# Working the first output projection by column pairs, with three and two groups of seven products for eight

## The reference

```python
merged = jax.nn.sigmoid(gate_a) * ya + jax.nn.sigmoid(gate_b) * yb
h = h + (merged @ w_out[l]).astype(h.dtype)
z = rmsnorm(h, norm_ffn_g[l])
ff = (jax.nn.silu(z @ w_ffn_gate[l]) * (z @ w_ffn_up[l])) @ w_ffn_down[l]
h = h + ff.astype(h.dtype)
```

## Time and profile before

| | us |
|---|---|
| three runs | 2528.5, 2528.8, 2529.35 |
| median | 2528.8 |
| profiled execution, span of its instructions | 2526.1 |
| PE busy in it | 2504.1 (99%) |
| DVE busy | 1874.6 (74%) |
| ACT busy | 1342.5 (53%) |
| POOL busy | 394.0 (16%) |

### The profile page before, as it was taken

How to read it: one execution, slowest core, us unless ns; L and a number is a source line. 1 busy time by engine, 2 the same in 40 slices (tenths; PEclk the granted TensorE clock), 3 DMA queues, 4 the chain that set the end, 5 groups by cost and what they waited for, 6 DMA issues and landing times.

```text
span 2526.1 us, 32950 instructions
## 1 busy us (share of the span) xinstructions
PE 2504.1 (99%) x11871; PEld 2103.8 (83%) x11871; DVE 1874.6 (74%) x2154; ACT 1342.5 (53%) x1801; POOL 394.0 (16%) x295
## 2 busy tenths in 40 slices
PE   9999999999999999999999999999999999999998
PEld 7889888888888888888789988888888888888887
DVE  5556554555799988999966766565669889988985
ACT  5445454444555555555555554455556655665564
POOL 1001100112212300212112301031132101210121
PEclk9999999999999999999999999999999999999999
DMA  7645556575656566565656655465465566556664
GB/s 243 201 145 156 168 168 191 191 238 179 225 192 203 188 207 226 193 201 194 227 182 183 182 148 157 149 217 175 158 220 190 194 209 207 198 199 205 211 213 161
DMA packets 252754, 485.98 MB, mean 192 GB/s; under 512 B 15339, under 2 KB 38844, under 8 KB 251468
## 3 DMA queue, kind: packets, MB, share of 16 engines
q1 hardware_dynamic: 248604, 463.99, 57.5%
q0 software_dynamic: 3696, 20.00, 2.1%
q10 hardware_dynamic: 320, 0.20, 0.0%
HBM read 478.86 MB, written 5.27 MB: 192 GB/s over the span
## 4 chain that ended last, share of the span: by engine, by line
PE 93%; DVE 3%; ACT 1%; issue 1%; DMA 0%; POOL 0%; ACTq 0%; DVEq 0%; POOLq 0%
PE acc L1667 73%; PE acc L1693 6%; PE unit L1693 4%; PE unit L1721 3%; PE psO L1693 2%; PE psS L1693 2%; PE psO L1895 1%; DVE w_lo L2023 1%; PE psS L1787 0%; ACT w_hi L1382 0%; PE psS L1861 0%; PE unit L1787 0%; DVE b_sum_lo L2215 0%; DMA w_raw<-in_w_o_cross 0%; POOL rtmp L1176 0%
## 5 line engine op out<-in xcount | busy, mean ns | idle before, releaser
L2023 DVE TENSOR_TENSOR w_lo<-w_raw,w_hi 128x1024 fp32r<-128x1024 f32 (+6 forms) x570 | 690.6, 1223 | 444.8 <-ACT w_hi L1382 439.6
L1382 ACT ACTIVATE w_hi<-w_raw 128x1024 fp32r<-128x1024 f32 (+6 forms) x570 | 573.3, 1016 | 429.1 <-PE acc L1667 401.2
L1667 PE MATMUL acc<-w_hi,xT_hi 128*128 128x512 f32 (+4 forms) x2020 | 783.1, 388 | 2.3 <-DVE xT_lo L2133 1.8
L1667 PE MATMUL acc<-w_lo,xT_hi 128*128 128x512 f32 (+4 forms) x2020 | 772.0, 382 | 0.0
L1667 PE MATMUL acc<-w_hi,xT_lo 128*128 128x512 f32 (+4 forms) x2020 | 771.4, 382 | 0.0
L1667 PEld LDWEIGHTS acc<-w_hi,xT_hi 128*128 128x128 f32 x2020 | 379.4, 188 | 71.3 <-issue 3.0
L1667 PEld LDWEIGHTS acc<-w_lo,xT_hi 128*128 128x128 f32 x2020 | 379.0, 188 | 70.0
L1667 PEld LDWEIGHTS acc<-w_hi,xT_lo 128*128 128x128 f32 x2020 | 379.6, 188 | 66.1 <-issue 0.5
L2054 DVE TENSOR_TENSOR w_lo<-w_raw,w_hi 128x1024 fp32r<-128x1024 f32 (+1 forms) x204 | 294.7, 1483 | 37.5 <-ACT w_hi L1411 36.3
L1411 ACT ACTIVATE w_hi<-w_raw 128x1024 fp32r<-128x1024 f32 (+1 forms) x204 | 200.1, 1018 | 106.6 <-PE acc L1667 92.4
L1667 PE MATMUL acc<-w_hi,hT_hi 128*128 128x512 f32 x632 | 247.3, 391 | 2.1 <-DVE w_lo L2023 1.4
(11 more groups left out here) (506 smaller groups left out, 3389.0 us busy)
## 6 DMA issues: line engine op xcount, KB each, us to landing
w_raw<-in_w_in SPq DMA_DIRECT2D x168, 512.0 KB, 3.7
w_raw<-in_w_down SPq DMA_DIRECT2D x110, 512.0 KB, 4.3
w_raw<-in_w_up SPq DMA_DIRECT2D x100, 512.0 KB, 4.1
w_raw<-in_w_ffn_down SPq DMA_DIRECT2D x76, 512.0 KB, 4.6
w_raw<-in_w_ffn_gate SPq DMA_DIRECT2D x68, 512.0 KB, 4.4
w_raw<-in_w_ffn_up SPq DMA_DIRECT2D x68, 512.0 KB, 3.8
w_raw<-in_w_out SPq DMA_DIRECT2D x64, 512.0 KB, 4.1
s_raw<-in_w_up SPq DMA_DIRECT2D x28, 512.0 KB, 6.0
```

The source lines that it names most:

```text
L1382: act.activation(w_hi[:, slot, 0:kc, 0:n], w_raw[:, slot, 0:kc, 0:n], ACT.Copy).then_inc(hi_split, 1)
L1667: ins = pe.matmul(ac[t][:, 0:n], a[:, l0 + c, t * P:(t + 1) * P], w[:, slot, c, 0:n], start=start and c == 0 and m == 0, stop=stop and c = ...
L2023: dve.tensor_tensor(w_lo[:, slot, 0:kc, 0:n], w_raw[:, slot, 0:kc, 0:n], w_hi[:, slot, 0:kc, 0:n].bitcast(F32), ALU.subtract).then_inc(lo_ ...
```

## The change

The four blocks of `w_out` become two pairs (columns 0 to 1023 and 1024 to 2047), with three groups of seven products in the first pair and two in the second. The products of a group read `xT` (new argument `lhs`). A new home `EARLY` has room for the sums of weights and activations and for the common parts. POOL makes the sums of the activations during the last `w_proj_b` block (`h_sums`), ACT and DVE split them after the first tile of `w_out` (`h_split`), and `merged3` is transposed after the fourth tile instead of the third. The loads of all five groups stay in the ring of four. Of the pair's common parts, 0 and 1 stand in pair one, 2 and 3 behind the second tile of pair two. The transposes `u0` and `u1` move behind tiles 8 and 10 of pair two's 12 plain tiles (counted from zero), `u2` and `u3` behind tiles 1 and 2 of the `w_ffn_gate` block. The home `START`, the step `shared_to` and blocks with `own` set are written but used by no step of this list.

```diff
+OUT = sevens((3, 2), ("0011S01S01S01", "01S01S00001111"), home=EARLY, ring=((0, 1, 2), (0, 1)), sums="dve", lhs="xT")
...
+    g = [group_of(OUT, half, 0, DC) for half in range(2)]
     for j in range(4):
         S += block_steps("w_proj_a", 0, 8, 512 * j, 512, "yT", 0, "gate_a", 512 * j, ("ya0", "ya1") if not j else ())
         S += weave(block_steps("w_proj_b", 0, 8, 512 * j, 512, "yT", 8, "merge", 512 * j, ("yb0", "yb1") if not j else ()),
-                   [[], both(f"merged{j - 1}")] if j else [], 1)
+                   [[("h_sums", g[0], 0)] if j == 3 else [], both(f"merged{j - 1}")] if j else [], 1)
     S += [("load_x",), ("gain", 2)]
     merged = tuple(f"merged{j}" for j in range(4))
-    blocks = [make_block("w_out", 0, DC, 512 * j, 512, "xT", 0, "add", 512 * j, () if j else merged) for j in range(4)]
-    sums_ = into_norm(2, blocks, {(3, 2): 0, (3, 4): 1, (3, 6): 2})
-    S += sums_[:3] + both("merged3") + sums_[3:]
...
+    one, rest = block_pair("w_out", 0, DC, 0, merged, 0, OUT["plans"][0], g[0], {0: [("h_split", g[0])], 3: both("merged3")})
+    two, more = block_pair("w_out", 0, DC, 1024, (), 0, OUT["plans"][1], g[1],
+                           {1: rest + pieces_of_norm(2, 0), 3: pieces_of_norm(2, 1), 8: both("u0"), 10: both("u1")})
+    assert not more
+    S += one + two + pieces_of_norm(2, 2) + pieces_of_norm(2, 3)
...
-    S += out_of_norm(2, make_block(*gate(0, U_NEEDS)))
+    first = make_block(*gate(0, U_NEEDS))
+    S += after_tiles([("tile", first, k) for k in range(8)], {0: roots(2), 1: both("u2"), 2: both("u3")}) + [("evac", first, (0, 1))]
...
                     if part == 0:
                         dve.wait_ge(p1_copied, at["group"])
+                        if group["home"] == EARLY and c0 == 0:
+                            dve.wait_ge(x_again_in, 16)
```

More of the change, by code:

```diff
@@ L244, in make_block @@
 def make_block(w, k0, kc, c0, n, lhs, l0, evac, arg=0, needs=(), turn=0):
-    return dict(w=w, k0=k0, kc=kc, c0=c0, n=n, lhs=lhs, l0=l0, evac=evac, arg=arg, needs=needs, norm=NORM_OF.get(w), ahead=0, turn=turn)
+    return dict(w=w, k0=k0, kc=kc, c0=c0, n=n, lhs=lhs, l0=l0, evac=evac, arg=arg, needs=needs, norm=NORM_OF.get(w), ahead=0, turn=turn,
+                own=False)
 def tiles_in(b):
@@ L256, in block_steps, with block_pair @@
     return [("tile", b, k) for k in range(tiles_in(b))] + [("evac", b, (0, 1))]
-def block_pair(w, k0, kc, c0, needs, turn, plan, group, between={}):
-    b = [make_block(w, k0, kc, c0 + 512 * j, 512, "hT", 0, "add", c0 + 512 * j, needs, turn) for j in range(2)]
+def block_pair(w, k0, kc, c0, needs, turn, plan, group, between={}, to=None):
+    what, arg = to or ("add", c0)
+    b = [make_block(w, k0, kc, c0 + 512 * j, 512, group["lhs"], 0, what, arg + 512 * j, needs, turn) for j in range(2)]
+    if to:
+        for x in b:
+            x["own"] = True
     plain = [k for k in range(kc // CK) if not 1 <= k <= group["n"]]
@@ L299, in weave @@
             n += 1
-            if n % every == 0 and slots:
+            if n >= every * (given + 1) and slots:
                 out += slots.pop(0)
+                given += 1
     for s in slots:
@@ L338, with group_of, with_sums @@
 U_NEEDS = ("u0", "u1", "u2", "u3")
+def group_of(plan, half, turn, kc):
+    first = (CK + turn) % kc
+    assert first + CK * max(plan["n"]) <= kc
+    return dict(n=plan["n"][half], summed=max(plan["n"]), l0=first, home=plan["home"], ring=plan["ring"][half], sums=plan["sums"],
+                lhs=plan["lhs"], clear=None)
+def with_sums(steps, group, units):
+    first = [i for i, s in enumerate(steps) if s[0] == "summed"][0]
+    i = [n for n, s in enumerate(steps[:first]) if s[0] == "tile"][-1]
+    return [("h_sums", group, units)] + steps[:i] + [("h_split", group)] + steps[i:]
 def schedule():
@@ L505, in number @@
     out, shapes, wrote, seen, apart, sevenths, held = [], {}, {}, {}, set(), {}, {}
-    c = dict(tile=0, lead=0, block=0, unit=0, split=0, hidden=0, seven=0, places=0, group=0, added=0, kept=0, back=0, after=2, relus=0, silus=0, sums=0, squares=0, root=0, gained=0)
+    c = dict(tile=0, lead=0, block=0, unit=0, split=0, hidden=0, seven=0, places=0, group=0, added=0, kept=0, back=0, after=2, relus=0, silus=0, sums=0, squares=0, root=0, gained=0, owned=0)
     ahead = 0
@@ L569, in number @@
             what = s[1]["evac"]
+            at["group"] = c["group"]
+            c["owned"] += 2 * (what == "qkva" and s[1]["own"])
             at["root"] = wrote.get(("root", 1))
@@ L609, in number @@
                 c["split"] += TRANSPOSES[s[1]][6] in ("split", "gain", "halves")
-            at["shared"] = c["group"] if c["after"] < 2 else None
+            at["shared"] = c["group"] if c["after"] < 2 and c["group"] else None
             c["after"] += 1
@@ L1327, in _ @@
                     pool.wait_ge(seven_done, at["seven"] + 1)
-                    pool.wait_ge(sums_kept, 32 * at["kept"])
-                    input_sums(hT, group["l0"], group["summed"], home["whole"], home["sum"])
+                    if at["kept"]:
+                        pool.wait_ge(sums_kept, 32 * at["kept"])
+                    input_sums(LHS[group["lhs"]], group["l0"], group["summed"], home["whole"], home["sum"])
                 elif s[0] == "sums_back":
@@ L1496, in _ @@
                     ac = acc[b % 2]
-                    if what == "ckv":
+                    if s[1]["own"]:
+                        for t in range(NT):
+                            v = own_view(s[1], t)
+                            if what == "sigB":
+                                block_read(act, at["block"], t)
+                                act.activation(v, v, ACT.Tanh, scale=stat[:, 6 + t:7 + t]).then_inc(sig_b_tanh, 1)
+                            else:
+                                act.wait_ge(own_added, at["owned"] + t + 1)
+                                act.activation(v, v, ACT.Copy, scale=over_rms(s[1]["norm"], t)).then_inc(acc_free[b % 2][t], 1)
+                    elif what == "ckv":
                         acc_ready(act, b, 0, last)
@@ L2147, in _ @@
                     ac = acc[b % 2]
-                    if what == "ckv":
+                    if s[1]["own"]:
+                        dve.wait_ge(shared_read, at["group"] + 1)
+                        for t in range(NT):
+                            acc_ready(dve, b, t, last)
+                            v = own_view(s[1], t)
+                            dve.tensor_tensor(v, v, like(s[1], ac[t][:]), ALU.add).then_inc(acc_free[b % 2][t] if what == "sigB" else own_added, 1)
+                    elif what == "ckv":
                         acc_ready(dve, b, 1, last)
```

56 lines of the change are left out of this document (40 added, 16 removed).

## The result

| | before | changed |
|---|---|---|
| median of 21 runs each, us | 2528.39 | 2532.46 |
| span of the profiled execution, us | 2526.1 | 2530.7 |
| PE instructions | 11871 | 11856 |

The ratio is 1.0017, with a 95% interval of 1.0012 to 1.0023: 4.1 us longer. The forecast was 1.6 us longer, so the sign came out and the size did not; 2532.46 lies in the upper part of the forecast's range.

What follows compares the result with a forecast made beforehand. PE's own work was taken to bound this stage. -3.40 + 4.0 + 0.9 + 0.1 = +1.6 us on the 2526.1 span gave 2527.7, with the median 2.7 above: 2530.4 us, range 2527.2 to 2534.2.

Steps and rivals of the forecast that it cites:

- What bounds, and what is removed: In this stage only PE's own work counts; five groups remove 15 matmuls, 3.40 us.
- the four terms: Removed matmuls -3.40, boundary gap +4.0, late second group +0.9, activations' sums on POOL +0.1: together +1.6 us.
- The boundary: At pair two's first group, PE waits for DVE's shared_read before starting psS: 3.9 to 4.5 us, taken as 4.0.
- T0: The end of pair one's third group, from which the prediction timed DVE's and PE's steps to the boundary.
- Nothing later recovers it: PE's boundary gap, taken as 4.0 us, is lost whole, as PE has no idle time behind it.
- The second group: Pair one's second group: late weight loads make PE wait for its first b_lo, 0 to 1.6 us, taken as 0.9.
- POOL's sums and the transposes: Activations' sums fit POOL's 19.11 us gap, slowing DVE 0 to 0.5 us, taken as 0.1; moved transposes cost nothing.
- The clock: Rival: the clock falls in the boundary gap, slowing the group's remaining 18 matmuls; 2 us more, 2532.4 us; chance 0.28.
- The likeliest case: Boundary gap alone, without a fall of the clock: 2529.3 to 2532.0 us, chance 0.45.
- DVE as the bound: Rival: in pair one, DVE's idle time beyond its spare 3.1 us becomes backlog at the boundary; 2534 to 2536, chance 0.15.

Runs made afterwards that it cites:

- e11: e10 with the 1 MB gain transfer moved into pair one, held until PE is through the first group; 2524.33 us, ratio 0.9986.
- e1: Changed kernel with part 2 of pair one's common parts put ahead of the weight sums of pair two's first group; 2532.56 us, ratio 1.0019.
- e8: Changed kernel with 18 more matmuls on PE ahead of the wait for shared_read, filling the idle gap; 2531.49 us, ratio 1.0014.
- e3: Changed kernel with the gain transfer alone held until PE is through pair one's second group; 2532.66 us, ratio 1.0018.
- e10: e2 with part 3, ACT's squares and POOL's gain products moved behind the sums of pair two's second group; 2526.18 us, ratio 0.9992.
- e12: e1 with ACT's squares of the first 512 columns behind pair two's second group's sums, the second 512 columns' steps one tile later; 2532.27 us.
- e2: Changed kernel with six plain tiles instead of four ahead of pair two's first group, part 2 behind the first tile, u0 and u1 later; 2530.63 us.

## Why the prediction was right or wrong

**What bounds, and what is removed: right.** 15 matmuls less, and 3.40 us, of which e11's stage gets 3.25. A wait on PE adds to the end: the four terms as measured make 4.97, the stage 4.81. (The 2.7 us put between span and median are 1.8 in every execution with both on record, 2532.48 against 2530.7 for one; the other 0.9 is what two executions can differ by.)

**The boundary: right in mechanism and size.** `shared_read` was put at T0 + 15.46; T0 was 565.37 and L2301 ended at 580.98, T0 + 15.61. The gap was put at 4.0 and is 4.11. The row-by-row walk of DVE's queue, taken from `w_ffn_down`, held.

**"Nothing later recovers it": right as a sum, wrong as a price.** Taking the gap and the low clock away (e1) gave back none of 6.8 us in the median and 0.5 in the trace; taking the low clock alone away (e8) gave back 1.0 and 0.7 of 2.7. The prediction's walk ends at "this group has no second stall"; it never took DVE from there to the next group. It would have met the squares on ACT and the products on POOL, which the change had put between the two groups behind part 3; the parts on the norm's transposes are in the prediction, these two are not. That POOL slows DVE was in its own rows (a `w_lo` of 1.88 instead of 1.22), but it was counted for the sums of the activations alone.

**The second group: mechanism right, size off.** 0.9 was taken from a range of 0 to 1.6; it is 1.54. The load had landed at 545.16, earlier than the 546.3 assumed:

```profile
545.16 1.06 ACT L1439 ACTIVATE w_hi<-w_raw 128x1024 fp32r<-128x1024 f32 x1 [4.71 <-DMA w_raw<-in_w_out]
...
550.72 0.50 PE L1750 MATMUL acc<-w_hi,x_sum_early_hi 128*128 128x512 f32 x1 [0.33 <-DVE w_lo L2076]
```

But the group's products waited three times (for `w_lo` and each `b_lo`), where the prediction has one wait, and each short wait cost PE more than its idle time (0.66 us idle in all, 1.54 lost). That the loads cause it is shown by e3 and e11.

**POOL's sums and the transposes: right.** No wait of PE stands there, though the split on DVE took 2.86 us instead of 1.75; e11 has the same places of the sums, and its transposes wait for nothing.

**The clock: the term that the sum left out.** The prediction named it as a rival of 0.28 and priced it at 2 us; it came, at 2.72. The likeliest case put it at nothing. The reading was that the fall comes about 3.8 us behind the last matmul, as long as the gap. Here it came sooner: PE's last matmul ended at about 577.1, and the slice 578 to 580 at 0.85 puts the fall at about 579.4. With 2.72 in the sum, and 1.54 for 0.9, the forecast would have been +4.96, where the stage is 4.81 longer and the median 4.1. But the clock alone is not why the likeliest case was too low. In e8 the clock stays at 1.00 and the stage is still 4.14 us longer than before: 18 matmuls in place of the gap, 1.4 us at pair one's second group, and 1.8 at pair two's second group, which the sum has nowhere. Without the clock's fall, the missing walk to that group would have shown instead.

**DVE as the bound: wrong place.** In pair one DVE idled 3.54 us at the load and still was on time: at T0 + 4 it waited for ACT, without backlog. It was the bound 20 us later, between the groups of pair two, and by POOL's slowing and ACT's order, not by its own sum of work. e10 shows it: the same DVE work, in another order of the list, leaves PE without a gap in pair two.

## What to carry to other kernels

A wait on the bounding engine has two prices: what it adds, and what comes back when it is taken away. For the second, walk the helpers' queues on to the *next* place where that engine needs them. Steps that an edit moves along with others (here the norm's squares and products behind part 3) need their own check of what they queue in front of, and what they run beside. And a transfer that is not due soon is best issued where no load is due, since moving it into another stretch only moves the wait.

## What was not expected of the hardware

- POOL's products of 512 columns in fp32 beside DVE's instructions with two inputs slow both: `w_lo` of 1024 from 1.22 to 2.31 us, sums of 512 from 0.69 to 1.67, and four products took 6.01 to 8.36 us, where two took 2.55 before.
- The granted clock is not told by one gap's length. In the gap of 4.1 us it fell 2.3 us behind the last matmul, at the end of the kernel 3.8 us behind it. In e12 a gap of 2.4 us (until 592.7) was followed by the lower level from about 594.4 to 597.8, when PE was already working. In e2 two gaps of 1.3 and 1.4 us with three matmuls between them brought it at about 587.3, and in e1 gaps of 0.9, 1.9 and 1.2 us, farther apart, did not. What decides between them stays open.
